# Two-layer decoder trunk on one core: the router reads raw sums, the first expert's tokens come from a product with a 0/1 matrix, and fillers run over the router's waits

## The reference, cut to what matters

```
h = x
for layer in range(2):
    u = rms_norm(h, mix_norm[layer])
    h = h + (even_mixer if layer == 0 else odd_mixer)(u, ...)
    h = h + hierarchical_moe(rms_norm(h, ffn_norm[layer]), ...)
return rms_norm(h, final_norm)

def hierarchical_moe(x2, ...):
    group_prob = softmax(x2 @ w_r1 + b_r1)            # 4 groups
    gp, gi = top_k(group_prob, 1)
    fine = (x2 @ w_r2 + b_r2).reshape(n_tok, 4, 8)    # 8 experts in a group
    ev, ei = top_k(fine of group gi, 2)
    gates = gp * softmax(ev)
    # every token goes to its 2 experts of 32:
    # y += gate * ((silu(x @ w_gate[e]) * (x @ w_up[e])) @ w_down[e])
```

## Time and profile before

| | before |
|---|---|
| median of three executions | 1942.1 us |
| the profiled execution: its own time | 1944.06 us |
| its span in the trace | 1942.3 us |
| PE busy | 1856.5 us (96%) |
| DVE busy | 1477.1 us (76%) |
| ACT busy | 1091.1 us (56%) |

### The profile page before, as it was taken

The page is one execution under the profiler, slowest core; times in us unless marked ns, Lnnn a source line. Parts: engine busy times, 40 slices in busy tenths (PEclk is TensorE's granted clock), DMA queues, the critical chain, the costliest instruction groups (busy, mean ns, idle before and its releaser), DMA issues.

```text
span 1942.3 us, 22709 instructions
## 1 busy us (share of the span) xinstructions
PE 1856.5 (96%) x8559; PEld 1390.9 (72%) x8565; DVE 1477.1 (76%) x1387; ACT 1091.1 (56%) x1059; POOL 267.9 (14%) x136
## 2 busy tenths in 40 slices
PE   6999979999999999999999999996999999999997
PEld 5876766777777777767787777784777777777775
DVE  4899657898989889895443535365889889888988
ACT  4225535777777777754221212234677777777774
POOL 0030001212221221200000000000122222222210
PEclk8999889999999999998999999997999999999998
DMA  7421037999999999994222222214899999999995
GB/s 264 174 87 44 17 140 263 359 366 361 369 375 370 367 367 370 367 348 164 92 80 87 87 87 87 87 44 172 329 370 372 369 366 360 365 365 364 368 372 201
DMA packets 77389, 494.93 MB, mean 255 GB/s; under 512 B 14745, under 2 KB 27033, under 8 KB 52624
## 3 DMA queue, kind: packets, MB, share of 16 engines
q1 hardware_dynamic: 60368, 467.68, 63.6%
q0 software_dynamic: 13888, 16.26, 2.5%
q10 hardware_dynamic: 3072, 10.18, 1.4%
HBM read 492.53 MB, written 34.08 MB: 271 GB/s over the span
## 4 chain that ended last, share of the span: by engine, by line
PE 87%; DVE 6%; issue 2%; ACT 2%; DMA 2%; SPq 0%; ACTq 0%; DVEq 0%; POOLq 0%
PE psum L857 12%; PE psum L858 12%; PE psum L862 12%; PE psum L776 8%; PE psum L777 8%; PE psum L778 8%; PE psum L879 6%; PE psum L880 6%; PE psum L883 6%; PE psum L846 3%; PE psum L1166 2%; DVE xs L1572 2%; PE psum L871 1%; DVE w_lo L651 1%; PE psum L785 1%
## 5 line engine op out<-in xcount | busy, mean ns | idle before, releaser
L651 DVE TENSOR_TENSOR w_lo<-raw,w_hi 128x2048 fp32r<-128x2048 f32 x384 | 863.2, 2289 | 138.4 <-ACT w_hi L661 136.7
L661 ACT ACTIVATE w_hi<-raw 128x2048 fp32r<-128x2048 f32 x384 | 713.8, 1911 | 29.7 <-DMA raw<-in_expert_w_up 18.8
L857 PE MATMUL psum<-w_hi,uT_hi 128*96 128x512 f32 x1024 | 406.6, 397 | 8.3 <-DVE uT_lo L1812 8.3
L858 PE MATMUL psum<-w_hi,uT_lo 128*96 128x512 f32 x1024 | 403.8, 394 | 0.0
L632 ACT ACTIVATE w_hi<-raw 128x2048 fp32r<-128x2048 f32 x46 | 87.8, 1913 | 345.1 <-PE psum L778 342.9
L862 PE MATMUL psum<-w_lo,uT_hi 128*96 128x512 f32 x1024 | 278.4, 394 | 0.0
L638 DVE TENSOR_TENSOR w_lo<-raw,w_hi 128x2048 fp32r<-128x2048 f32 x46 | 105.3, 2290 | 211.8 <-ACT w_hi L632 208.1
L2091 POOL DMA_INDIRECT y_dram<-y_e,index x60 | 131.4, 2190 | 823.7 <-DVE y_e L1829 782.9
L857 PEld LDWEIGHTS psum<-w_hi,uT_hi 128*96 128x96 f32 x1024 | 168.5, 165 | 75.0 <-DVE uT_lo L1812 9.3
L862 PEld LDWEIGHTS psum<-w_lo,uT_hi 128*96 128x96 f32 x1024 | 166.2, 162 | 70.4
L2085 POOL DMA_INDIRECT x_e<-xs_dram,index x64 | 120.0, 1875 | 699.1 <-DVE index L1805 643.2
(11 more groups left out here) (212 smaller groups left out, 2270.2 us busy)
## 6 DMA issues: line engine op xcount, KB each, us to landing
raw<-in_expert_w_gate SPq DMA_DIRECT2D x64, 2048.0 KB, 9.9
raw<-in_expert_w_up SPq DMA_DIRECT2D x64, 2048.0 KB, 11.0
raw<-in_expert_w_down SPq DMA_DIRECT2D x64, 2048.0 KB, 10.0
raw<-in_odd_w_in SPq DMA_DIRECT2D x8, 2048.0 KB, 8.6
raw<-in_odd_w_in SPq DMA_DIRECT2D x8, 1024.0 KB, 8.2
raw<-in_odd_w_out SPq DMA_DIRECT2D x4, 2048.0 KB, 7.8
raw<-in_even_w_in SPq DMA_DIRECT2D x3, 2048.0 KB, 10.3
raw<-in_even_w_in SPq DMA_DIRECT2D x4, 1024.0 KB, 12.4
```

The source lines that it names most:

```text
L651: nc.vector.tensor_tensor(part(w_lo[b]), src, part(w_hi[b]).bitcast(F32), ALU.subtract).then_inc(m.lo[b], 1)
L661: nc.scalar.activation(part(w_hi[b]), src, ACT.Copy).then_inc(m.hi[b], 1)
L857: nc.tensor.matmul(psum[0:r, bank], xeT_hi[:, c, 0:r], hi[:, j], start=(half + j == 0), stop=False)
L858: nc.tensor.matmul(psum[0:r, bank], xeT_lo[:, c, 0:r], hi[:, j], start=False, stop=False)
```

## The change

The router's transposes read `h` instead of `xs`, so they no longer wait for the norm. The gain is multiplied into `wr` once, early, on DVE (a new input `gain_t`, 8 KB); the reciprocal root is multiplied onto the logits in `route`. PE turns tile q - 1 behind tile q of the last projection (`turn_sums`). The first expert's turned tokens no longer come from a gather: DVE makes `first_oh` (tokens by 96 slots, one small operation for each tile of 128 tokens), and PE multiplies `xs` by it, 32 float32 matmuls that land turned in the two banks which the transposes of `x_e` used. The table, the lists and the gather of expert 1 stand behind that, the `slot_gate` product stands behind expert 0's up product, and the gates of rows stand behind the copy of expert 1's tokens. `warm` puts matmuls whose result nobody reads in PE's order: 50 ahead of the wait for `chosen`, 8 ahead of the wait for `first_ok` and 8 behind the table. On ACT, layer 1's split of the second gate half and the store of `xs` change places with the logits' copies. `plan_banks` fixes banks 5, 6 and 7 for the router's later jobs, which moves the turn for the jobs that follow.

```diff
 def plan_banks():
...
-            if q and layer is not None:
-                b.plan(("logitsT", layer, q - 1))
+            if q == 2 and layer is not None:
+                b.plan(("logitsT", layer, 0))
...
-    b.plan(("logits", 0))
-    b.plan(("pos", 0))
-    b.plan(("table", 0))
-    b.plan(("slot_gate", 0))
+    b.plan(("logits", 0), 5)
+    b.plan(("pos", 0), 6)
+    b.plan(("table", 0), 7)
     b.before_experts = [list(b.uses)]
+    b.plan(("slot_gate", 0), 7)
...
+            def turn_sums(layer, q):
+                copied(pe, *(("out1", R_HEADS - 1, 1, q) if layer else ("out0", 1, q)))
+                turn_rows(2 * layer + 1, q, h[:, q])
+
+            def warm(dst, times):
+
+                for _ in range(times):
+                    nc.tensor.matmul(dst[:, 0:2 * P], ones, count_w.rearrange("p a t -> p (a t)"), start=True, stop=True)
...
             def moe(layer):
                 m, past = main, EXPERTS * layer
-                pe.wait_ge(const_in, 16 * N_CONST)
-                norm(2 * layer + 1, layer)
+                pe.wait_ge(eps_ok, 3)
+                router_logits(layer, 0)
+                turn_sums(layer, TILES - 1)
+                for q in range(1, TILES):
+                    router_logits(layer, q)
...
                 dst, full = open_bank("pos", layer)
+                pe.wait_ge(count_ok, layer + 1)
+                warm(dst, WARM[0])
                 pe.wait_ge(chosen, layer + 1)
...
+                warm(table_at, WARM[1])
+                pe.wait_ge(first_ok, layer + 1)
+                for c in range(KC):
+                    for q in range(TILES):
+                        mm = nc.tensor.matmul(psum[:, c // 4, (c % 4) * P:(c % 4) * P + FIRST],
+                                              xs[:, q * DM + c:(q + 1) * DM:KC], first_oh[:, q],
+                                              start=(q == 0), stop=(q == TILES - 1))
+                mm.then_inc(m.xT_psum, 1)
                 pe.wait_ge(placed, 2 * layer + 1)
...
+                warm(psum[:, 2], WARM[2])
+                copied(pe, "pos", layer)
+                copied(pe, "table", layer)
...
-                pe.wait_ge(m.gathered[0], 16 * (past // 2 + 1))
-                transpose_tokens(m, 0)
...
                     up_product(pairs, 3, s % 2, m.up_half, m.up_psum, ready)
+                    if type(e) is int and e == 0:
+                        gates_of_slots()
...
             def route(layer):
                 src, free = bank("logits", layer)
                 V.tensor_tensor(logit, src[:, 0:TILES * NROUT].rearrange("p (q n) -> p q n", q=TILES),
-                                br[:, layer].unsqueeze(1).broadcast_to([P, TILES, NROUT]), ALU.add).then_inc(free, 1)
+                                stat[:, 12:16].unsqueeze(2).broadcast_to([P, TILES, NROUT]), ALU.mult).then_inc(free, 1)
                 copied(dve, "logits", layer)
+                link(V.tensor_tensor(logit, logit, br[:, layer].unsqueeze(1).broadcast_to([P, TILES, NROUT]), ALU.add))
...
+                link(V.tensor_copy(pos, src[:, 0:TILES * EXPERTS].rearrange("p (q n) -> p q n", q=TILES)))
+                for q in range(TILES):
+                    ins = V.tensor_scalar(first_oh[:, q], slot_no[:, 0:FIRST], pos[:, q, 0:1], in_first[:, q:q + 1],
+                                          ALU.is_equal, ALU.mult)
+                ins.then_inc(first_ok, 1)
...
                 route(layer)
                 if not layer:
                     dve.sem_inc(m.y_dve, 1)
                 copy_tokens(m, past + 1, 0)
+                lists(layer)
                 moe_split(dve, layer, "up", 0, 0, True, (0, 1) if layer else (1,))
...
                         copy_tokens(m, e + (past + 2), (s + 1) % 2)
+                        gates_of_rows(layer)
...
-                gather(m, 0, 0)
                 gather(m, 1, 1)
```

More of the change, by code:

```diff
@@ L208, in plan_banks @@
     norm(3, 1)
-    b.plan(("logits", 1))
-    b.plan(("pos", 1))
-    b.plan(("table", 1))
-    b.plan(("slot_gate", 1))
+    b.plan(("logits", 1), 5)
+    b.plan(("pos", 1), 6)
+    b.plan(("table", 1), 7)
     b.before_experts.append(list(b.uses))
+    b.plan(("slot_gate", 1), 7)
     last_rows(1)
@@ L910, in moe @@
                 mm.then_inc(full, 1)
-                dst, full = open_bank("table", layer)
+                table_at, table_full = open_bank("table", layer)
+                late = {banks.at(name, layer)[0] for name in ("pos", "table")}
+                for b in range(8):
+                    if b not in late:
+                        pe.wait_ge(bank_free[b], banks.before_experts[layer][b])
+                warm(table_at, WARM[1])
[5 more added lines that the diff above has]
+                                              start=(q == 0), stop=(q == TILES - 1))
@@ L918, in moe @@
-                pe.wait_ge(placed, 2 * layer + 2)
-                for k in range(TOPK * TILES):
-                    mm = nc.tensor.matmul(dst[:, 0:2], oh[:, k, 0:P].bitcast(F32), last_gates[:, k], start=(k == 0),
-                                          stop=(k == TOPK * TILES - 1))
-                mm.then_inc(full, 1)
-                for b in range(8):
-                    pe.wait_ge(bank_free[b], banks.before_experts[layer][b])
-                pe.wait_ge(m.gathered[0], 16 * (past // 2 + 1))
@@ L1782, in route, with gates_of_rows @@
                 make_lists(0, 1, link, index_ok)
+            def gates_of_rows(layer):
+                gates = gate.rearrange("p k q -> p (k q)")
                 dve.wait_ge(index_ok, layer + 1)
```

115 lines of the change are left out of this document (68 added, 47 removed).

## The result

The kernel with the change takes **1953.5 us** (median of 4 runs, 1951.49 to 1956.73) against 1942.9 us for the kernel before beside it (4 runs, 1941.19 to 1944.01). The ratio is 1.0057, with a 95% interval of 1.0045 to 1.0069: 10.6 us slower, where the prediction had 14.3 us faster. The profiled execution took 1953.13 us, with a span of 1951.3. Some executions of these kernels take about 37 us more at a lower mean clock (the traces of e7 and e18 show some 85 us at clock 0.50 ahead of layer 0's router), and they are left out of all ratios.

What follows compares the result with a forecast made beforehand. PE bounds the kernel, with time to win only where it waits or runs slower, mainly the router's serial chain through DVE. Layer 0's 4.6, layer 1's 7.5 and the banks' 2.2 sum to 14.3 us: 1927.8 us, range 1923 to 1934.

Steps and rivals of the forecast that it cites:

- the product with `first_oh`: PE ahead of expert 0: 64 records at 0.117 us each, 7.5 us, range 7.4 to 9.3.
- The full clock at the gate product: Expert 0's first gate product was expected at the full clock, winning 2.3 us more.
- Table and last fillers in the gap: PE has table and fillers between the product and expert 0, so the full clock was expected there.
- Start of expert 0: Layer 0's first gate product at 287.7 instead of 291.86, 4.2 us earlier.
- Layer 1, 7.5 us: Layer 1 given layer 0's times: first product 7.7 us earlier, 7.5 us by the second expert.
- The 50 fillers: Ahead of `chosen` on PE: 0.117 us each, 5.9 us in all, ending even with `chosen`.
- Raw sums: Router transposes of raw sums drop the 0.80 us wait for `xs`; `both` ends 0.46 us earlier.
- The banks: At `norm(2)`, waits for additions to `h` go: 2.2 us, down to 0 if another wait steps in.
- The gather of expert 1: Lists and gather for expert 1 come later, behind expert 0's first product's copies; costed at nothing.
- The dip at the second expert: Behind the second expert's start, a low clock losing 1.6 us, counted in one layer, which one unknown.
- The rival of the clock: Clock falls despite fillers, product takes 14.2 us: 1951.8 us; decides from 0.229 us a record; chance 4%.
- The rival of loads that don't overlap: Small matmuls' weight loads don't overlap: fillers cost 5 us and product 4.7 us a layer, 1947 us; chance 2%.

Runs made afterwards that it cites:

- e7: Changed kernel with `xs` ordered by chunk, `gain_p` at the arena's end and 64-byte padding around the first two `w_hi`/`w_lo` pairs: 1929.83 us, ratio 0.9911.
- e18: Changed kernel, but the `first_oh` product loads `xs` at steps of 2, 3 and 1 elements, giving expert 0 wrong channels: 1974.46 us, one run.
- e12: Kernel before, with only `xs` and the gains of the two routed norms ordered by chunk: 1931.55 us, ratio 0.9948.
- e1: Changed kernel, but the `first_oh` product loads 128 neighbouring columns of `xs`, giving expert 0 wrongly ordered channels: 1931.85 us, ratio 0.9947.
- e4: Kernel before, with bank numbers from `norm(2)` on starting at bank 0 instead of 4: 1939.74 us, ratio 0.9987.
- e6: Changed kernel with the new columns `gain_p` at the arena's end, so tiles behind `stat` keep their former addresses: 1953.46 us, ratio 1.0050.
- e15: Kernel before, with 64 unused bytes ahead of `stat`: 1943.98 us against 1943.74, ratio 1.0004.
- e9: Changed kernel with `xs` and the routed norms' gains ordered by chunk and `gain_p` at the arena's end: 1922.39 us, ratio 0.9890.
- e14: As e9, with 64 fillers instead of 50 ahead of the place count in layer 1 alone: 1917.76 us, ratio 0.9871.

## Why the prediction was wrong

**The step that failed** is the product with `first_oh`: "64 records ... I take 0.117 since weights and engine state are the same: 7.5 us", with bounds of 0.115 and 0.145. It took 15.57 us, 0.238 a record. The row at 258.18 did load the same columns, but for transposes of 128 moved columns, which start some 0.11 us apart whether the load is strided (`xs`) or contiguous (`prob`), so that the strided load did not show; with 96 columns moved it does (0.111 against 0.082, e12). The other row, L802, was a two-record float32 product, but it loads 36 neighbouring columns of `wr` (128 neighbouring ones cost no more, 0.112 in e1). I joined the two and took their common price; the product needed 128 strided columns in a two-record product, which no row showed. That its records cost twice the transposes' fits two reads of the weights a record; this is argued, not shown. There was a clue within reach: in the trace of the kernel before, the transposes of `x_e` move 96 columns instead of 128 and start as far apart, and their loads take 201 ns against 145 for the contiguous ones of `prob`:

```profile
L846 PEld LDWEIGHTS psum<-square,x_e 96*128 96x128 f32 x512 | 67.1, 201 | 12.7 <-issue 5.7
L1084 PEld LDWEIGHTS psum<-square,prob 128*128 128x128 f32 x80 | 9.1, 145 | 13.6 <-issue 12.8
```

**What followed from it**, in the prediction's own steps:

- *The full clock at the gate product* (2.3 a layer): lost. The fillers did hold 1.00 up to the product, and the product lost it 5 us in. With fast records (e1) it held, and the gate product took its 5.5 us.
- *Table and last fillers in the gap* (nothing): they ran at half clock, and 8 fillers of 1.89 us ended 0.9 behind DVE's copy of the table. PE's own fillers were late.
- *Start of expert 0* at 287.7: it came at 295.27. In e1 it came at 284.34, in a trace that ran 2.3 us ahead of the kernel before at the first logits; 286.6 by that clock.
- *Layer 1, 7.5 us*: its part ahead of the place count came (5.5 us by raw sums and the moved split, where I had 4.0), and was lost to the product.

**What was right.** The 50 fillers took 5.63 us (5.9). `first_oh` took 1.05 us for four, 0.26 each, above my 0.15 and within the range. The slot products took 1.7 us (1.9). Raw sums gave 1.8 us in layer 0 where I had 0.46: too small. The banks gave what they should (e4), and of their 2.2 us the changed kernel shows 1.6 between the layers. The gather of expert 1 cost nothing. The dip at the second expert came in both layers (313.0 to 316.4 and 1364.3 to 1367.7 at clock 0.50), not in one.

**What was not in the prediction at all.** The experts' period: 0.1 us for two experts from 64 bytes, 3.1 us by the traces. Whether the time pays for it stays open: twice (e6, e15) the period moved by that and the time did not. Why the address matters stays open. Open too is why the clock fell in the slow records and not in the fast ones.

The rival of the clock had almost the right total (1951.8) by luck, with the wrong cause: it let the clock raise the record to 0.222. Its own mark, "decides from 0.229 us a record", was passed by the stride alone. The rival of loads that don't overlap named the right engine part: it is the loads that bound these records, but not since they fail to overlap: loads of 335 ns stand in records 0.238 us apart, and in e1 loads of 192 ns in records 0.112 us apart.

With what was measured in place of those terms: forecast 1927.8; the product 8.1 more in each layer, 16.2; table and fillers 1.0 a layer; gate product 2.0 a layer; the second dip 1.6: 1951.6. The period adds 3.1, raw sums take 1.3 and 1.5 away: 1951.9, against 1953.5 measured, with falls of the clock elsewhere of that size.

## What to carry to other kernels

Look at the step of whatever TensorE loads, not only at what it moves: lay tiles out so that the loaded operand is contiguous, even if DVE pays 0.4 us more for a strided write (`hid`) or 0.8 for a strided read (the norm). That is worth it where DVE has the time; ahead of layer 1's router it cost 1.4 us and a fall of the clock (e9). Before taking a record's price from another row, match the operation, the step of the loaded operand and the number of records for each product; if two rows each match half, the bounds must reach to twice the dearer one. And where rows of different width cost the same (96 and 128 columns at 0.11 us), ask what else bounds them: here that question was worth more than the whole change.

## What the runs showed of the hardware

- A record of a float32 product with 128 loaded and 96 moved columns costs 0.112 us with contiguous weights, 0.118 at a step of 2, 0.177 at 3, 0.233 at 4, 0.238 at 8; the last two don't depend on the granted clock.
- TensorE's clock fell from 2.4 to 1.2 GHz while the trace showed PE busy for all of it (276.75 to 282.00, 22 records in 5.25 us). It did not fall with 64 records in 7.38 us in the same place. A busy PE by the trace is not one that holds its clock.
- Float32 transposes of 96 moved columns start 0.111 us apart with a strided load and 0.082 with a contiguous one; that alone took 10 us off the kernel before (e12).
- A pause of 1.81 us between fillers and place count was followed by a fall of the clock within 1.3 us of the count's start, and with 14 more fillers in the pause the clock held (e9, e14).
- 64 bytes of shift in the weights' tiles change a long row of matmuls by 0.3% (35.67 and 35.77 us for two experts), cause unknown.
